# Decoder layer with routed experts: token rows stored unnormalised and scaled behind the gather, two gathers ahead of the branch, a sixth chunk split early

## The reference

```python
h = h + mixer_block(rms_norm(h, norm1[l]), ...)
h = h + hier_moe(rms_norm(h, norm2[l]), moe_wrg[l], moe_brg[l], moe_wre[l], moe_bre[l],
                 moe_wg[l], moe_wu[l], moe_wd[l])
return rms_norm(h, norm_f)

def hier_moe(x, w_rg, b_rg, w_re, b_re, w_g, w_u, w_d):   # x: (512, 1024)
    g_logits = xt @ w_rg + b_rg                # 4 groups; the best one is taken
    e_logits = (xt @ w_re + b_re).reshape(-1, 4, 4)
    # the best two experts of that group; weights: softmax over both, times the group's probability
    for e in range(16):
        h = silu(xt @ w_g[e]) * (xt @ w_u[e])  # w_g, w_u: 1024 x 512
        out = out + gates[:, e:e+1] * (h @ w_d[e])   # w_d: 512 x 1024
```

## Time and profile before

| what | us |
|---|---|
| median of 3 runs | 913.15 |
| lowest, highest | 908.6, 914.84 |
| profiled execution | 911.01 |
| its span, first to last instruction | 909.1 |
| PE, DVE, ACT, POOL busy | 838.4, 660.1, 475.4, 88.0 |

### The profile page before, as it was taken

The page is one execution under the profiler, slowest core; times in us unless marked ns, Lnnn a source line. Parts: engine busy times, 40 slices in busy tenths (PEclk is TensorE's granted clock), DMA queues, the critical chain, the costliest instruction groups (busy, mean ns, idle before and its releaser), DMA issues.

```text
span 909.1 us, 19485 instructions
## 1 busy us (share of the span) xinstructions
PE 838.4 (92%) x8314; PEld 556.0 (61%) x8314; DVE 660.1 (73%) x934; ACT 475.4 (52%) x678; POOL 88.0 (10%) x90
## 2 busy tenths in 40 slices
PE   5999999999999998999999999939899989988882
PEld 4444784845856554444444469919788678777651
DVE  4759599799756787444435355566799999998987
ACT  5433673322666654232332335534778878788742
POOL 8000000002000000000000000010222313122000
PEclk9999999999999999999999999957999999999996
DMA  9732023434961115934234254465899999999972
GB/s 243 176 93 70 2 71 94 116 94 116 229 183 36 42 39 171 352 105 128 85 107 118 79 148 182 153 254 198 324 356 395 400 379 402 386 384 373 379 285 96
DMA packets 122641, 178.29 MB, mean 196 GB/s; under 512 B 13373, under 2 KB 98677, under 8 KB 114358
## 3 DMA queue, kind: packets, MB, share of 16 engines
q1 hardware_dynamic: 116272, 162.76, 52.5%
q0 software_dynamic: 6000, 13.67, 5.7%
q10 hardware_dynamic: 278, 0.56, 0.2%
HBM read 170.73 MB, written 14.39 MB: 204 GB/s over the span
## 4 chain that ended last, share of the span: by engine, by line
PE 62%; DVE 14%; DMA 13%; ACT 7%; issue 4%; POOLq 0%; ACTq 0%; POOL 0%; SPq 0%; DVEq 0%
PE bank L1044 19%; PE bank L1046 18%; PE bank L1045 18%; DVE arena L1887 5%; DMA arena<-in_moe_wu 3%; DMA arena<-in_moe_wd 3%; DMA arena<-x_rows,token_of 3%; ACT arena L914 2%; PE bank L1162 1%; PE bank L1275 1%; DVE arena L2002 1%; DMA arena<-y_rows 1%; DMA x_rows<-arena 1%; ACT arena L999 1%; DMA y_rows<-arena,row_of 1%
## 5 line engine op out<-in xcount | busy, mean ns | idle before, releaser
L1045 PE MATMUL bank<-arena 128*128 128x96 f16 (+4 forms) x2488 | 527.7, 258 | 0.0
L1044 PE MATMUL bank<-arena 128*128 128x128 f16 (+6 forms) x1976 | 456.7, 271 | 16.2 <-DVE arena L1887 6.5
L1046 PE MATMUL bank<-arena 128*128 128x128 f16 (+6 forms) x1976 | 455.5, 270 | 0.0
L1045 PEld LDWEIGHTS bank<-arena 128*128 128x128 f16 (+1 forms) x2488 | 248.7, 100 | 66.5 <-issue 0.7
L1044 PEld LDWEIGHTS bank<-arena 128*128 128x128 f16 (+2 forms) x1976 | 197.0, 100 | 110.4 <-issue 24.2
L1046 PEld LDWEIGHTS bank<-arena 128*128 128x128 f16 (+2 forms) x1976 | 196.4, 100 | 77.3 <-issue 0.7
L1887 DVE SCALAR_TENSOR_TENSOR arena<-arena 128x2048 f16<-128x2048 f32 x94 | 213.1, 2287 | 33.0 <-ACT arena L914 32.9
L914 ACT ACTIVATE arena<-arena 128x2048 f16<-128x2048 f32 x94 | 176.0, 1907 | 15.1 <-DMA arena<-in_moe_wu 7.6
L663 ACT ACTIVATE arena<-arena 128x1024 f16<-128x1024 f32 (+1 forms) x91 | 91.4, 1008 | 101.8 <-PE bank L1046 68.5
L1581 DVE SCALAR_TENSOR_TENSOR arena<-arena 128x1024 f16<-128x1024 f32 (+1 forms) x91 | 104.2, 1162 | 12.2 <-ACT arena L663 10.9
L1044 PE MATMUL bank<-beat,arena 128*128 128x96 f16 x512 | 72.1, 213 | 4.1 <-DVE arena L1887 4.0
(11 more groups left out here) (293 smaller groups left out, 770.8 us busy)
## 6 DMA issues: line engine op xcount, KB each, us to landing
arena<-in_moe_wg SPq DMA_DIRECT2D x32, 1024.0 KB, 18.0
arena<-in_moe_wu SPq DMA_DIRECT2D x32, 1024.0 KB, 19.6
arena<-in_moe_wd SPq DMA_DIRECT2D x32, 1024.0 KB, 20.0
arena<-in_w_gate SPq DMA_DIRECT2D x32, 512.0 KB, 3.8
arena<-in_w_in SPq DMA_DIRECT2D x31, 512.0 KB, 3.8
arena<-in_w_branch SPq DMA_DIRECT2D x32, 192.0 KB, 3.4
y_rows<-in_c_tab SPq DMA_DIRECT2D x4, 1024.0 KB, 11.3
arena<-in_w_out SPq DMA_DIRECT2D x8, 512.0 KB, 3.9
```

Source lines behind the costliest of these rows:

```text
L1044: pe.matmul(outb, lhs[0], rhs[0], start=first, stop=False, skip_group_check=True)
L1045: pe.matmul(outb, lhs[0], rhs[1], start=False, stop=False, skip_group_check=True)
L1046: return pe.matmul(outb, lhs[1], rhs[0], start=False, stop=last_, skip_group_check=True)
```

## The change

- **Rows.** `hg` is stored unnormalised to `x2_rows`, one column block after another during the output product, on SP's queue between the loads of chunks 10 to 14. The scaling of all rows (L942) and their store (L519) go.
- **Scale behind the gather.** `x_transposes` multiplies the gathered rows by a diagonal matrix with the tokens' factors (`slot_diag`) instead of by the identity. For experts 0 and 1 the factors come with the token numbers from the one-hot product (`near_told`), and VectorE makes the diagonals. From expert 2 on, POOL gathers the factors from HBM with a second indirect DMA (`rslot`, one number a slot), waits for both and makes the diagonal itself. SP stores the factors (512 numbers) once.
- **Order.** Gathers 0 and 1 stand ahead of the branch on POOL, each with a buffer of its own. A sixth chunk (`PRE`) is split ahead of the branch, and SP loads chunk 15 ahead of it. In the loop over steps both splitting engines split chunk c+5 at the beginning of turn c, where it had been near the end. The tokens of expert 1 are transposed after step 0 (before: step 3), those of expert 2 after step 8 (before: 7). The list of all slots is made in turn 3 (before: 4) and the big one-hots and the experts' weights after the branch.
- **Routing.** One signed comparison replaces two and a product and a maximum; one comparison against two thresholds replaces two. Missing slots are marked by subtracting 1024 in the table itself. The near experts' one-hots are made one at a time in fp32 straight from the ranks in PSUM; the big ones cover 96 places where they had covered 128. The root's table is loaded in turn 6 of the output product. `WARM` is 6.

```diff
-WARM = 12
+WARM = 6
+PRE = 1
-NOWHERE = 65536
+NOWHERE = 2 * T
@@ x_at
-            if e + 1 < NE and hf and kind == ("u" if e < NEAR else "g"):
+            if c == 0:
+                return 1
+            if c == STEPS.index(("d", 0, 0)):
+                return 2
+            if NEAR <= e < NE - 1 and hf and kind == "g":
                 return e + 1
@@ SP
+            for m in range(KD):
+                sp_.wait_ge(S("hg_ready"), m + 1)
+                sp_.dma_start(x2_rows[:, m * P:(m + 1) * P].rearrange("(t p) n -> p t n", p=P), hg[:, :, m * P:(m + 1) * P]
+                              ).then_inc(S("x2_stored"), 16)
+                for i in SPLIT_AT.get(m - 1, ()):
+                    sp_.wait_ge(S("split_done"), splits_ahead(READY + i))
+                    stage_load(READY + i)
+            sp_.wait_ge(S("out_full"), KD)
+            for c in (READY - 2, READY - 1):
                 stage_load(c)
-            for t in range(NT):
-                sp_.wait_ge(S("x2_ready"), t + 1)
-                sp_.dma_start(x2_rows[t * P:(t + 1) * P, :], xs[:, t, :]).then_inc(S("x2_stored"), 16)
+            sp_.wait_ge(S("rstd2_ready"), 1)
+            sp_.dma_start(rstd_rows((1, P), (P, NT), (1, 1)), rstd2.unsqueeze(2),
+                           allow_slow_non_contiguous=True).then_inc(S("rstd_stored"), 16)
+            sp_.wait_ge(S("token_read"), NEAR)
+            stage_load(READY + FIRST)
@@ POOL
+            pool.wait_ge(S("x2_stored"), 16 * KD)
+            pool.wait_ge(S("token_read"), 1)
+            gather_rows(0)
+            pool.memset(xg[1], 0.0).then_inc(S("pool_step"), 1)
+            pool.wait_ge(S("pool_step"), 5)
+            pool.wait_ge(S("token_read"), 2)
+            gather_rows(1)
             pool.wait_ge(S("path_known"), 1)
@@
+                        pool.wait_ge(S("xgT_full"), 2 * e)
+                        if e == NEAR:
+                            pool.wait_ge(S("token_read"), NEAR + 1)
+                            pool.wait_ge(S("rstd_stored"), 16)
+                        gather_rows(e)
+                        pool.indirect_dma_start(out=rslot[0:CAP, e:e + 1], out_offset=None, in_=rstd_rows((1, T), (1, 1)),
                                                 in_offset=bass.IndirectOffsetOnAxis(ap=token_of[0:CAP, e:e + 1], axis=0),
                                                 bounds_check=T - 1, oob_is_err=False).then_inc(S("xg_landed"), 16)
+                        pool.wait_ge(S("xg_landed"), rows_landed(e))
+                        pool.tensor_scalar(slot_diag[e % 2][0:CAP, :], ident[0:CAP, 0:CAP], rslot[0:CAP, e:e + 1], None, ALU.mult
+                                           ).then_inc(S("slot_diag"), 1)
@@ ACT
+                if m == KD - 2:
+                    link(act.activation(stat[:, 2, 0:1], ones[:, 0:1], ACT.Sqrt))
@@
-            for t in range(NT):
-                act.activation(xs[:, t, :], hg[:, t, :], ACT.Copy, scale=stat[:, 3, t:t + 1]).then_inc(S("x2_ready"), 1)
+            act.wait_ge(S("hgT_used"), KD)
+            for i in range(FIRST, FIRST + PRE):
+                split(i)
@@ ACT and DVE, at the head of turn c (before: behind the turn's output copy)
+                    if FIRST + PRE <= c + LOOK < CUT:
+                        split(c + LOOK)
@@ PE
                 def x_transposes(e):
-                            last = pe.transpose(ps[6 + j][:, k * CAP:(k + 1) * CAP], xg[0:CAP, 4 * P * j + k:4 * P * (j + 1):4],
-                                                ident[0:CAP, 0:CAP])
+                            last = pe.matmul(ps[6 + j][:, k * CAP:(k + 1) * CAP], x_gathered(e)[0:CAP, 4 * P * j + k:4 * P * (j + 1):4],
+                                             slot_diag[e % 2][0:CAP, :], start=True, stop=True)
@@ DVE
-            link(tt(tied, other, own, ALU.is_ge))
-            link(tt(ahead, other, own, ALU.is_gt))
-            link(tt(tied, tied, lower.rearrange("p (i j) -> p i j", j=EPG).unsqueeze(1).to_broadcast(wide), ALU.mult))
-            link(tt(ahead, ahead, tied, ALU.max))
+            link(tt(lead, other, own, ALU.subtract))
+            link(tt(ahead, lead, beaten_by.rearrange("p (i j) -> p i j", j=EPG).unsqueeze(1).to_broadcast(wide), ALU.is_ge))
@@
+            sig("onehot_ready", tt(*near_views(0), ALU.is_equal))
+            dve.wait_ge(S("rank_full"), 2)
+            for e in range(NEAR):
+                dve.wait_ge(S("token_full"), e + 1)
+                sig("token_read", ts(token_of[0:CAP, e:e + 1], near_token(e)[:, 0:1], float(NOWHERE), None, ALU.add))
+                link(dve.tensor_copy(rslot[0:CAP, e:e + 1], near_token(e)[:, 1:2]))
+                if e + 1 < NEAR:
+                    sig("onehot_ready", tt(*near_views(e + 1), ALU.is_equal))
+                tell("slot_diag", ts(slot_diag[e][0:CAP, :], ident[0:CAP, 0:CAP], rslot[0:CAP, e:e + 1], None, ALU.mult))
+            for i in range(FIRST, FIRST + PRE):
+                split(i)
@@ DVE, behind the branch
                 x_lo(0)
                 for c, (kind, e, hf) in enumerate(STEPS):
-                    if c == 4:
+                    if c == 0:
+                        for t in range(NT):
+                            tell("onehot_ready", tt(*onehot_views(t), ALU.is_equal))
+                        x_lo(1)
+                    if c == 3:
                         all_slots()
```

More of the change, by code:

```diff
@@ L176, in constants @@
     sq[:, 3 * P:3 * P + 4] = r[:, None] + P * np.arange(NT)[None, :]
-    sq[:, 3 * P + 4:3 * P + 20] = np.tril(np.ones((EPG, EPG)), -1).reshape(-1)
+    sq[:, 3 * P + 4:3 * P + 20] = np.where(np.tril(np.ones((EPG, EPG)), -1), 0.0, np.finfo(np.float32).tiny).reshape(-1)
+    sq[:, 3 * P + 20:3 * P + 40] = np.repeat([0.5, 1.5], [EPG, NE])
     for h in range(IDX_HEADS):
@@ L180, in constants @@
             sq[n % 16 + 64 * (n // 16), NCST + IDX_DIM * h + n] = 1.0
-    half = np.zeros((P, 2 * P), np.float16)
-    half[:, 0:P] = r[:, None] < r[None, :]
+    half = np.zeros((P, 2 * P + CAP), np.float16)
+    half[:, 0:P] = (r[:, None] < r[None, :]) - float(NOWHERE) * np.eye(P)
     half[:, P:2 * P] = 1.0
-    numbers = np.repeat(np.arange(P, dtype=np.float16), NE)[None, :]
+    half[:, 2 * P:] = np.arange(CAP) - NOWHERE
+    numbers = (np.repeat(np.arange(P), NE) - NOWHERE).astype(np.float16)[None, :]
     n = T + P
@@ L406, in build, with near_token, rows_landed, rstd_rows @@
         scratch, x2_rows, y_rows = d["bias_scratch"], d["x2_rows"], d["y_rows"]
+        def near_token(e):
+            return ps[7][0:CAP, 2 * e:2 * e + 2]
+        def rows_landed(e):
+            return 16 * (1 + 2 * max(e + 1 - NEAR, 0))
+        def rstd_rows(*shape):
+            return bass.AP(scratch.tensor, 0, list(shape))
         def y_bank(e):
@@ L538, in _ @@
             with sp_.Else():
-                for i in range(READY):
+                for i in range(READY + 1):
                     sp_.wait_ge(S(f"stage_landed{i}"), 32 if i < FIRST else 16)
-                sp_.wait_ge(S("split_done"), FIRST)
-                sp_.wait_ge(S("token_full"), 1)
+                sp_.wait_ge(S("split_done"), FIRST + PRE)
+                sp_.wait_ge(S("xg_landed"), 16)
+                sp_.wait_ge(S("xg1_landed"), 16)
+                sp_.wait_ge(S("x2_stored"), 16 * KD)
+                sp_.dma_start(hg_dense, x2_rows.rearrange("(t p) n -> p t n", p=P)).then_inc(S("xres_landed"), 16)
                 for e in range(NE):
@@ L609, in _ @@
             with pool.If(fit):
-                for n in range(ROUTED + 3):
+                for n in range(NEAR, ROUTED + 3):
                     if n == 4:
@@ L1422, in _ @@
                         else:
-                            pe.wait_ge(S("token_read"), 2)
-                    if kind == "g" and not hf:
-                        pe.wait_ge(S("xlo_done"), 2 * (e + 1))
-                        if e >= 2:
+                            pe.wait_ge(S("token_read"), NEAR + 1)
+                    if kind == "g":
+                        pe.wait_ge(S("xlo_done"), 2 * e + hf + 1)
+                        if e >= 2 and not hf:
                             pe.wait_ge(S("h_ready"), e - 1)
@@ L1483, in _ @@
                     for t in range(NT):
-                        last = pe.transpose(b[:, t * P:(t + 1) * P], xs[:, t, c * P:(c + 1) * P], ident)
+                        last = pe.matmul(b[:, t * P:(t + 1) * P], hg_dense[:, t, c * P:(c + 1) * P], dense_diag[:, t, :],
+                                         start=True, stop=True)
                     main_full(last)
@@ L2038, in _ @@
+                    if FIRST + PRE <= c + LOOK < CUT:
+                        split(c + LOOK)
+                    if c == 1:
+                        tell_lists()
+                    if c and x_at(c):
                         x_lo(x_at(c))
@@ L2073, in _ @@
                 new_chain("dve_step_body", before)
+                weights()
+                for t in range(NT):
+                    tell("diag_ready", ts(dense_diag[:, t, :], ident, rstd2[:, t:t + 1], None, ALU.mult))
```

192 lines of the change are left out of this document (89 added, 103 removed).

## The result

| | before | after |
|---|---|---|
| median, us | 912.42 | 940.39 (4 runs, 934.26 to 942.24) |
| ratio to before, 95% interval | | 1.0306 (1.0279 to 1.0332) |
| profiled execution's span, us | 909.1 | 939.8 |

The kernel became 28 us slower; the forecast was 902 us, with 912 as the upper end of its range. Executions more than 1.5% above the fastest of their kernel stay out of the ratios; in this document that is two, of the version with 128-column lists. Routing and the token numbers come about as worked out. From the landing of the first gather on, the times don't.

What follows compares the result with a forecast made beforehand. VectorE was taken to pace the middle and loads the end. VectorE's 14.5 us gain less 1.9 for the last scatter and 2 where both lines meet, taken as 11, came off 913.15: 902.0 us, 8-in-10 range 895 to 912.

Steps and rivals of the forecast that it cites:

- A diagonal product in fp32 costs what the transpose does: PE, gathered tokens of every expert: 275 ns a product against a mean of 299 for transposes, so no added cost.
- What ends last there. ScalarE and VectorE, not PE: Before the first expert product: VectorE's arithmetic to 602.7, then ScalarE's branch; product near 605.7, a gain of 8 us.
- the 64 list products, 4.1 us: PE, early expert phase: list products take 4.1 us and end at 622.4; expert 2's token numbers come at 624.
- 2.5 for both: POOL, from expert 2 on: factor gather and diagonal product together add 2.5 us after the row gather's landing.
- the estimate beside the sum: Factor gather from expert 2 on: about 2.0 us fixed by the skill page, hidden wholly, 2 us better at expert 3.
- POOL's cycle becomes the bound: Rival, middle of the expert phase: POOL's cycle of 18 us over nine experts loses 18 us, giving 920; chance 0.12.
- scatters more than 16.1 apart: Sign in the expert phase: such spacing from the start would mean that POOL's cycle is the bound.
- Landing 4.6 to 5.5 later: Gather 0, ahead of the branch: issued at 596.2, landing 4.6 to 5.5 us later, near 601.
- 1.9 later: Kernel's end: the last expert's output copy stands behind a 1.90 us split, so the last scatter comes 1.9 us later.
- sum at the end: Whole kernel: the later of VectorE's and the loads' lines counts; 14.5 - 1.9 - 2 = 10.6, taken as 11 us.
- VectorE's line: From expert 3 to the end: 9.5 us ahead plus 5 formerly lost to loads after 800 makes 14.5.
- loads' line: DMA from 617 us to the end: 4 + 14.8 - 3.5 = 15.3 us gained; as a rival, 898 us, chance 0.11.

Runs made afterwards that it cites:

- the version with all three parts taken back: Kernel after with transposes by the identity, 128-column list products and no factor gather or POOL diagonal (tokens unscaled): 906.53 us, 0.9955 of the kernel before.
- chunk 15 and the second store held: Kernel after, 128-column lists, experts 2 to 15 transposed from normalised rows stored a second time; that store waits for gather 0, chunk 15 for expert 1's transposes: 905.90 us.
- the version with chunks 8 and 9 held as well: The version with normalised rows stored a second time after gather 0 landed, with loads 8 and 9 issued only behind that store: 905.02 us, 0.9928 of the kernel before.

## Why the prediction was wrong

**The step that failed first** is "A diagonal product in fp32 costs what the transpose does: 275 ns ... This edit is free at every expert." reads x64, but L1099 makes 32 products: x64 counts instructions, two for each fp32 product, where the earlier trace rows has 128 for 128 transposes. I compared one duration with another and not one product with one transpose. And that row's columns lie side by side, where x_transposes takes every fourth. The term put at 0 measured 43.7 us on PE's line, and taking it out gave 25.3 us at the end of the kernel. I had asked whether PE ends last only at the first product ("What ends last there. ScalarE and VectorE, not PE"); for the middle I never worked out how much PE had free. It stood in the earlier trace rows: 93.27 of 100 us.

**The lists** ("now 96 of 128 places: 3.5" for VectorE, "the 64 list products, 4.1 us" for PE). VectorE's term was right: the one-hots took 3.55. PE's took its duration from rows with 128 columns and gave it to loads of 96: 11.7 us. `row_of`, forecast at 624, was written at 638.91, later than the 634.17 of before; VectorE idled 9.57 us for it. In the version with all three parts taken back it came at 628.99.

**POOL's gather and product.** The gather was dearer in the sum than in fact: 2.5 for both, where the gather alone moved nothing. It landed 7.2 us after its issue in the median (3.1 to 8.4), not 2.0 as in the estimate beside the sum, and cost nothing all the same with PE full. The product had the wrong price because I priced it alone: 0.53 to 7.99 us, by what VectorE is doing. The rival "POOL's cycle becomes the bound" is nearest in sign but isn't what happened: its scatters stay 17.11 apart with POOL's part gone. So my own sign for it, "scatters more than 16.1 apart", didn't tell POOL from PE. No rival had PE as the bound.

**The first gather.** It was issued at 597.67, 1.5 after the 596.2 that I had, ahead of the branch as meant. "Landing 4.6 to 5.5 later" failed: 8.94, and 10.10 in the version with all three parts out. So PE began at 606.66, and the first expert product came at 610.50, 3.1 earlier than before instead of 8. With chunk 15 and the second store held it lands in about 4.3, and the first product is at 607.53, against 604.9 to 607 forecast; the rest is ScalarE's branch, met at 604.61 where I had 602.7. What delays the landing wasn't isolated, but the rows narrow it. Chunks 8 and 9 don't: they are issued at 588.96 in the run that lands in 4.3. The 6.21 with chunks 8, 9 and 15 held isn't a queue's time either: the DMA share is 0.01 or less from 598 to 602, and 3.25 of the 6.21 are POOL's own row, which began together with a VectorE split (1.05 in the kernel after). That leaves chunk 15 and a store that the sum left out, the 512 single factors:

```profile
590.40 0.65 SPq L555 DMA_DIRECT2D bias_scratch<-near_told  x1
```

It takes 13.1 us to land, to about 603.5, and from 598 to 604 the DMA engines are busy 0.58, 0.79 and 0.35 of the time (in steps of 2 us) while they move only 37 to 55 GB/s. The version that lands in 4.3 has no such store. No run held this store or chunk 15 alone.

**The place of the splits** ("1.9 later") had the sign wrong: going back costs 2.1, and the last output shows no delay from it.

**What held.** Routing starts at 591.14 (forecast 590.8, before 591.57). The token numbers of experts 0 and 1 come at 596.53 and 598.99 (595.9 and 598). The "sum at the end" can be read against the version with all three parts taken back, whose gain is 4.1 us by the ratio where I had 11. VectorE's line nearly held at its start: expert 3's tokens start at 652.99 against 659.50, 6.5 ahead, with 17 low-half splits done instead of 16, so 8.8 by the prediction's count (9.5 there). The loads' line is the term that failed. From 617 to 640 us the loads ran at 253 GB/s against 246, which is 0.4 of the 8.6 us counted there (less the 3 to 4 that I took as lost); from 640 to 700 they ran at 385 against 353, 4.9 of 6.2. Between 800 and 860 ScalarE waits for them as long as before (13.1 against 13.7 us), so the 5 us that VectorE's line was to win there didn't come: the scatters are 5.3 ahead from the second to the sixth and 4.6 at the last. Why the loads up to 640 us stayed slow no run isolates; in the version with chunks 8 and 9 held as well they ran at 307 GB/s.

## What to carry to other kernels

Price an edit by what it issues, with type, width and step of the columns, and count instructions for each piece of work in the row that you borrow from. For each engine, write down its free time per turn in the stage that sets the pace before calling an edit free there: here PE had 1.1 us, and 2.7 us more per expert became 15 to 25 at the end. Ask, too, what stands behind the delay: here a stretch paced by the loads took in up to 8 us of it, as long as PE wasn't full there. A small operation on POOL beside long VectorE splits has no price of its own; if PE waits for it, give it to an engine that doesn't stand in that line, or do the scaling once ahead.

## What the hardware showed that I had not expected

- An fp32 weight load of 128 columns from 96 partitions took 209 ns in the mean with neighbouring columns and 328 ns with a step of four. The transposes' loads with the same step took 216.
- A weight load of 96 fp16 columns (step of 16) took 277 ns, one of 128 columns 164 to 169, at a granted clock of 1.00 and of 0.50 alike.
- POOL's indirect DMAs show the same long rows as its product. The scatter in the version with chunks 8, 9 and 15 held took 6.79 us from 736.21, beside a run of VectorE splits. In the kernel before, a gather issued at 720.15 took 4.83 us and VectorE's two splits there 4.48 from 719.66. There POOL had time for it.
- A store of 512 single fp32 numbers took 13.1 us to land with chunks 8 and 9 issued ahead of it, and 8.9 with both held.
- POOL's part is worth 9.6 us with PE full and 2.6 with PE relieved. Undoing one part says what it costs in those surroundings only.
